# Expert slots in halves by token tile: two row halves of the array sum side by side, empty slots are not gathered

## The chip, the cores and the metric

One core of one Trainium2 chip. The metric is the device time of one execution in microseconds (us), the median over the runs of a kernel. Batch 1, 512 tokens of 1024 numbers behind 16 learned meta tokens, all in fp32.

## What is computed

One block of a hybrid encoder: input layer norm, a combined projection with two recurrent branches, output projection and layer norm, then the mixture of experts, which the change touches:

```python
scores = jax.nn.sigmoid((xt @ router_w).astype(jnp.float32))
_, idx = jax.lax.top_k(scores + router_bias, TOP_K)              # 6 of 64 experts
s_sel = jnp.take_along_axis(scores, idx, axis=-1)
wts = s_sel / jnp.sum(s_sel, axis=-1, keepdims=True) * ROUTED_SCALE
y = sum over the 6 of  wts_e * ((silu(x @ w_gate_e) * (x @ w_up_e)) @ w_down_e)  + swiglu(xt, ws_...)
h = layer_norm(DEEPNORM_ALPHA * h + y, ln2_g, ln2_b)
```

D_EXPERT is 256, so an expert has 3 MiB of weights (gate and up 1024x512, down 256x1024), and all are read. 512 x 6 = 3072 (token, expert) assignments are made.

## The kernel before

The kernel runs in four stages. The front (to some 515 us of the profile) is the projection and the two branches and isn't touched but for where small tiles lie. Routing (`out_and_route`, 515 to 609 us) makes the output projection, the norm, the shared expert (L1010, L1024) and the plan of the experts. The experts (`experts`, 609 to 1157 us) are a loop. The last norm stands at the end.

**Items and slots.** Work on experts is cut into items of 64 slots (SLOTS). An expert gets one item, and a further one for each 64 tokens beyond the first 64. Two items make a pair (PAIR): their 128 slots are the 128 partitions. Pairs run one after the other, three buffers deep (THIRDS); a pair is called p. The loop's body (`one` on each engine) is written three times and runs `n_rounds` times.

**Routing.** A token's place within its expert is a running count over all tokens (L1047 and L1048 on PE, bank PO). DVE turns places and counts into `pw`, the number of further items (L1181 to L1187), and then into tables for 112 possible items: `slot_of` (which slot a token has in an item, L1204) and `table` (three bf16 parts of the weight and two of the token number, L1211 to L1213). PE fills the time with the shared expert. The first look-up (L838) needs the table, the shared down projection (L1024) needs `shared_aT` (L1192), which stands behind the table on DVE.

**A pair in the loop.** In the order in which PE has it:
- `gate_up` (L1298): 16 matmuls of 512 columns in fp32, two items side by side, each in 64 columns of the array. Each fp32 matmul has two records in the profile (two passes), so 32.
- `turn_x` (L864): 8 transposes of the gathered rows `xg` of the next pair. ACT copies them (L872).
- `turn_a` (L1307): 2 transposes of the activations.
- `scatter` (L1322, L1323): the outputs of the pair before are added up by token. ST (128 slots x 512 tokens, ones and zeros, built by DVE at L1405) is the stationary operand: for each of 4 token tiles t and each half m of the columns, one matmul of y_hi and one of y_lo (fp32r, one pass) into one of five PSUM banks (SUM). DVE adds each of the 8 sums into `acc` (L1416) and gives the bank back (`sum_free`). The fourth sum also waits for `xgT_ready`, since its bank is one that the transposes used.
- `look_up` (L838): 4 small bf16 matmuls that find token number and weight of the slots of pair p + 3. DVE sums them up (L846 to L851, `look_free`, `idx_ready`).
- `down` (L1331): 8 fp32 matmuls of 512 columns, two items side by side in 64 columns each, 16 records.

GpSimd gathers 128 rows of 4 KiB for pair p + 3 from `h1_rows` in memory with an indirect DMA (L857). A slot without a token has token number 0 and weight 0: row 0 is fetched for it. SyncE loads the weights, six DMAs of 1 MiB for a pair (L776), each as soon as `gate_up` or `down` of the pair three before has freed its place.

After the loop a last scatter runs; ACT makes total and squares of each token tile when it is summed (L1392, L1394), DVE normalises (L1474, L1478), and SyncE stores.

## Time and profile before

| | us |
|---|---|
| median of three runs | 1182.53 |
| the three runs | 1187.83, 1182.53, 1177.49 |
| the profiled execution | 1177.19 |
| its span (first to last instruction) | 1175.4 |
| granted TensorE clock, mean | 0.994 |
| PE busy | 1128.4 (96%) |
| DVE busy | 744.1 (63%) |
| DMA read and written | 248 GB/s over the span, 420 GB/s in the loop |

A line of the profile names the line of the kernel, engine, operation and tiles, then the number of records. PE is TensorE's matmuls, PEld its weight loads. Ends of matmuls are modelled: the start of the next one tells how long one held the array. Transfers are not part of an engine's busy time. The chain of waits is the path back from the last instruction.

### The profile page before, as it was taken

What the parts mean: (1) busy time and instruction counts of PE and PEld (TensorE: products, weight loads), DVE (VectorE), ACT (ScalarE), POOL (GpSimd) and SP (SyncE); (2) the same over time, 40 slices, a digit from 0 to 9 for tenths busy, and PEclk for the clock granted to TensorE, in tenths of its full rate; (3) what the DMA queues carried; (4) which work ended last, traced back from release to release, by engine and by line L of the source; (5) the groups of instructions that cost most, each with busy time, mean ns of one, the idle gap of its engine ahead of it and who ended that gap; (6) DMA issues with size and microseconds to landing.
All of it is one profiled execution on the core that took longest, in us unless ns stands there. A gap on an engine that the chain in (4) does not pass through costs nothing.

```text
span 1175.4 us, 17834 instructions
## 1 busy us (share of the span) xinstructions
PE 1128.4 (96%) x6340; PEld 726.2 (62%) x6340; DVE 744.1 (63%) x1253; ACT 443.0 (38%) x692; POOL 204.7 (17%) x108
## 2 busy tenths in 40 slices
PE   5999999999999999999999999999999999999993
PEld 4878888888888888646544444444444454444441
DVE  8868585858586867674544555555555555555557
ACT  7656565766575657302002122211221122211224
POOL 1433242424243424100010000000000000000000
PEclk9999999999999999999999999999999999999997
DMA  6121212212121303139179999999999999999981
GB/s 235 43 107 47 102 61 86 74 74 90 57 103 44 122 26 132 47 130 400 70 314 421 419 420 422 420 421 421 421 421 421 421 421 421 422 420 421 421 352 71
DMA packets 48294, 292.08 MB, mean 248 GB/s; under 512 B 7680, under 2 KB 9088, under 8 KB 16528
## 3 DMA queue, kind: packets, MB, share of 16 engines
q1 hardware_dynamic: 43088, 272.91, 56.9%
q0 software_dynamic: 5184, 18.88, 4.0%
q8 instruction: 13, 0.21, 0.1%
q14 instruction: 9, 0.07, 0.0%
HBM read 287.57 MB, written 4.19 MB: 248 GB/s over the span
## 4 chain that ended last, share of the span: by engine, by line
PE 53%; DVE 1%; DMA 1%; ACT 1%; issue 0%; DVEq 0%; POOLq 0%
PE pair L1298 20%; PE pair L1331 11%; PE pair L1322 5%; PE pair L1323 5%; PE pair L864 3%; PE pair L1010 2%; PE pair L162 2%; PE pair L1307 1%; DMA xg<-h_rows,idx 1%; PE pair L1003 1%; DVE acc L1474 0%; ACT first L1394 0%; PE pair L997 0%; PE pair L838 0%; PE pair L1024 0%
## 5 line engine op out<-in xcount | busy, mean ns | idle before, releaser
L368 PE MATMUL pair<-hT,w_parts 128*128 128x264 f32 (+1 forms) x2112 | 376.2, 338 | 2.0 <-DVE hT L628 1.6
L368 PEld LDWEIGHTS pair<-hT,w_parts 128*128 128x128 f32 x2112 | 319.9, 188 | 47.9 <-issue 4.1
L215 POOL TENSOR_TENSOR w_parts<-w_raw,w_parts 128x1024 fp32r<-128x1024 f32 x66 | 167.2, 2535 | 307.0 <-ACT w_parts L209 295.5
L1416 DVE TENSOR_TENSOR acc<-acc,pair 128x512 f32<-128x512 f32 x280 | 170.6, 682 | 32.5 <-PE pair L1323 32.5
L1298 PE MATMUL pair<-raw,xgT 128*64 128x512 f32 x768 | 168.9, 592 | 0.0
L857 POOL DMA_INDIRECT xg<-h_rows,idx x36 | 33.9, 942 | 596.6 <-DVE idx L851 596.6
L1377 ACT ACTIVATE y_hi<-pair,w_now 128x512 fp32r<-128x512 f32 x70 | 48.1, 687 | 208.9 <-PE pair L1331 208.9
L1298 PEld LDWEIGHTS pair<-raw,xgT 128*64 128x64 f32 x768 | 55.1, 137 | 109.8 <-issue 109.8
L1408 DVE TENSOR_TENSOR act_a<-act_s,pair 128x256 f32<-128x256 f32 x35 | 14.7, 421 | 168.2 <-ACT act_s L1370 168.2
L1322 PE MATMUL pair<-y_hi,ST 128*128 128x512 f32 x280 | 112.6, 402 | 1.6 <-DVE y_lo L1429 1.6
L1323 PE MATMUL pair<-y_lo,ST 128*128 128x512 f32 x280 | 109.4, 391 | 0.0
L1370 ACT ACTIVATE act_s<-pair 128x256 f32<-128x256 f32 x35 | 13.4, 383 | 219.9 <-PE pair L1298 219.9
L1331 PE MATMUL pair<-raw,aT 128*64 128x512 f32 x384 | 87.7, 598 | 0.0
L1429 DVE SCALAR_TENSOR_TENSOR y_lo<-pair,w_now,y_hi 128x512 fp32r<-128x512 f32 x70 | 52.6, 751 | 43.0 <-ACT y_hi L1377 31.1
L1298 PE MATMUL pair<-first,xgT 128*64 128x512 f32 x352 | 77.4, 592 | 0.0
L209 ACT ACTIVATE w_parts<-w_raw 128x1024 fp32r<-128x1024 f32 x67 | 70.3, 1050 | 0.0
L1322 PEld LDWEIGHTS pair<-y_hi,ST 128*128 128x128 f32 x280 | 52.7, 188 | 12.8 <-DVE y_lo L1429 2.5
L1323 PEld LDWEIGHTS pair<-y_lo,ST 128*128 128x128 f32 x280 | 52.7, 188 | 10.1
L162 PE MATMUL pair<-w_raw,merged 128*128 128x512 f32 x128 | 55.6, 593 | 1.8 <-DVE acc L1125 1.6
L1298 PEld LDWEIGHTS pair<-first,xgT 128*64 128x64 f32 x352 | 25.3, 137 | 50.2 <-issue 50.2
L864 PEld LDWEIGHTS pair<-ident,xg 128*128 128x128 f32 x288 | 34.9, 194 | 30.4 <-issue 30.4
L695 DVE SCALAR_TENSOR_TENSOR xc<-xr,par,xc 128x528 f32<-128x528 f32 x24 | 51.8, 2157 | 0.6
(269 smaller groups left out, 1287.9 us busy)
## 6 DMA issues: line engine op xcount, KB each, us to landing
raw<-in_w_gate_up SPq DMA_DIRECT2D x96, 1024.0 KB
raw<-in_w_down SPq DMA_DIRECT2D x48, 1024.0 KB
first<-in_w_gate_up SPq DMA_DIRECT2D x44, 1024.0 KB, 25.7
w_raw<-in_w_in SPq DMA_DIRECT2D x36, 1024.0 KB, 6.7
first<-in_w_down SPq DMA_DIRECT2D x22, 1024.0 KB
xin<-in_x SPq DMA_DIRECT2D x4, 512.0 KB, 5.2
ws_gu<-in_ws_gate_up SPq DMA_DIRECT2D x1, 2048.0 KB, 7.8
h_rows<-acc SPq DMA_DIRECT2D x4, 512.0 KB, 21.1
```

Of the source, the lines that this page charges most:

```text
L162: return pe.matmul(banks[2 * (t % 2) + n][:, :], mem["merged"][:, j, t * P:(t + 1) * P], mem["w_raw"][:, j // 2, j % 2, n * 512:(n + 1) * ...
L209: act.activation(w[:, n % PARTS, 0], w_raw[:, n // 2, n % 2], ACT.Copy).then_inc(sem("w_hi_ready"), 1)
L215: pool.tensor_tensor(w[:, n % PARTS, 1], w_raw[:, n // 2, n % 2], w[:, n % PARTS, 0].bitcast(F32), ALU.subtract).then_inc(sem("w_lo_ready" ...
L368: last = pe.matmul(o, w[:, n % PARTS, pw, k * P:(k + 1) * P], hT[ph][:, k, of], start=(k == 0 and m == 0), stop=(k == KB - 1 and m == 2))
L695: ins = v.scalar_tensor_tensor(xc[:], xr[:, i:i + TA], c(C_W0 + i), xc[:], ALU.mult, ALU.add)
L864: last = pe.transpose(self.XT[k // 4][:, (k % 4) * P:(k % 4 + 1) * P], self.xg[b][:, k::KB], self.mem["ident"][:])
L1298: last = pe.matmul(GU[half[s], :], xgT[:, (KB // 2) * c + k, half[s]], w[s][:, k * 2 * F:(k + 1) * 2 * F], start=(c == 0 and k == 0), stop ...
L1322: pe.matmul(o, st, y_hi[:, m * 512:(m + 1) * 512], start=True, stop=False)
L1323: pe.matmul(o, st, y_lo[:, m * 512:(m + 1) * 512], start=False, stop=True)\
L1331: last = pe.matmul(Y[m][half[s], :], aT[:, j, half[s]], w[s][:, j * D + m * 512:j * D + (m + 1) * 512], start=(j == 0), stop=(j == 1))
L1416: v.tensor_tensor(part, part, SUM[g % len(SUM)], ALU.add).then_inc(sem("sum_free"), 1)
L1429: v.scalar_tensor_tensor(y_lo[:, cols], Y[m], w_now[:, 0:1], y_hi[:, cols].bitcast(F32), ALU.mult, ALU.subtract).then_inc(sem("y_ready"), 1)
```

## The change

**Halves.** The 64 slots of an item become a lower and an upper half of 32 (HALF). Places count up from 0 in the lower half, and from UPPER = 1024 in the upper one. A token of the first token tile (t = 0) always lies in a lower half, one of the last (t = 3) always in an upper half; tiles 1 and 2 fill what is left. The items of an expert are as many as the largest of its tokens / 64, its tokens of tile 0 / 32 and its tokens of tile 3 / 32 ask for, rounded up. `items_of` works that out on DVE, from three counts that PE makes with five more matmuls into TOT, and again for the count of items (own_tot). Possible items become 136 instead of 112.

**Order of the slots.** A pair's 128 partitions are now half by half: 32 lower slots of item 0, 32 lower of item 1, then the two upper. The transposes write their columns in an order that puts an item's 64 slots side by side again for `gate_up`, and `turn_a` turns them back. `down` therefore works on four groups of 32 columns of the array (16 matmuls, 32 records) instead of two of 64.

**Scatter.** Tile 0 needs only the partitions 0 to 63 of ST and y, tile 3 only 64 to 127. Their sums are matmuls over 64 rows each, issued in turns (SUMS: tile 0 LOW beside tile 3 HIGH, for m = 0 and m = 1). Tiles 1 and 2 stay as they were. Sums are made and reported two by two (`sum_done` += 2 behind the last of four matmuls), and the wait for `xgT_ready` is at the third sum instead of the fourth. The token tiles end in the order 0, 3, 1, 2 (TILES).

**Empty slots.** Token numbers are kept with FAR = 4096 subtracted; FAR is added at the end, so an empty slot has index 4096, and the gather, which now has a bounds check, leaves it out. GpSimd clears the three `xg` buffers once, during routing.

**Look-up.** DVE multiplies the looked-up numbers with a mask of whose slots they are and makes three operations over 128 partitions of what were four over 64. `build` is two operations of half the width.

```diff
-EXTRA = T * TOP_K // SLOTS
+HALF = SLOTS // 2
+EXTRA = 2 * P * TOP_K // HALF + (T - 2 * P) * TOP_K // SLOTS
...
     def build(self, v, b, item):
-        v.tensor_tensor(self.Sb[b][:], row.broadcast_to([P, TT, PAIR, SLOTS]),
-                        at.broadcast_to([P, TT, PAIR, SLOTS]), ALU.is_equal).then_inc(self.sem("S_built"), 1)
+        for h in range(2):
+            row = self.mem["iota"][:, h * HALF:(h + 1) * HALF].rearrange("p (t u s) -> p t u s", t=1, u=1)
+            v.tensor_tensor(self.Sb[b][:, :, h], row.broadcast_to([P, TT, PAIR, HALF]),
+                            at.broadcast_to([P, TT, PAIR, HALF]), ALU.is_equal).then_inc(self.sem("S_built"), 1)
...
-        for s in range(PAIR):
-            v.tensor_reduce(self.idx_f[b][half[s], :], GU[half[s], s * TAB + 3:s * TAB + TAB], AX, ALU.add)\
-             .then_inc(sem("idx_summed"), 1)
-        v.tensor_reduce(self.w_next[b][half[0], :], GU[half[0], 0:3], AX, ALU.add)
-        v.tensor_reduce(self.w_next[b][half[1], :], GU[half[1], TAB:TAB + 3], AX, ALU.add).then_inc(sem("look_free"), 1)
-        v.wait_ge(sem("idx_summed"), PAIR * p + PAIR)
-        v.tensor_copy(self.idx[b][:], self.idx_f[b][:]).then_inc(sem("idx_ready"), 1)
+        v.tensor_tensor(self.looked, GU[:, 0:PAIR * TAB].rearrange("p (u n) -> p u n", u=PAIR), self.of_item,
+                        ALU.mult).then_inc(sem("look_step"), 1)
+        v.wait_ge(sem("look_step"), 2 * p + 1)
+        v.tensor_reduce(self.idx_f[b], self.looked[:, :, 3:TAB], mybir.AxisListType.XY, ALU.add)\
+         .then_inc(sem("look_step"), 1)
+        v.tensor_reduce(self.w_next[b], self.looked[:, :, 0:3], mybir.AxisListType.XY, ALU.add)\
+         .then_inc(sem("look_free"), 1)
+        v.wait_ge(sem("look_step"), 2 * p + 2)
+
+        v.tensor_scalar(self.idx[b], self.idx_f[b], FAR, None, ALU.add).then_inc(sem("idx_ready"), 1)
...
         pool.indirect_dma_start(self.xg[b][:], None, self.mem["h1_rows"],
-                                bass.IndirectOffsetOnAxis(ap=self.idx[b][:, 0:1], axis=0))\
+                                bass.IndirectOffsetOnAxis(ap=self.idx[b], axis=0),
+                                bounds_check=T - 1, oob_is_err=False)\
...
+        for n, of in numbers:
+            for t in of:
+                last = pe.matmul(TOT[:, n * E:(n + 1) * E], ones[:], chosen[:, t, 0], start=(t == of[0]), stop=(t == of[-1]))
...
+        def items_of(to, n012, n3, n0):
+            st(v.tensor_tensor(to, n012, n3, ALU.add))
+            st(v.scalar_tensor_tensor(to, to, 0.5, n0, ALU.mult, ALU.max))
+            st(v.tensor_tensor(to, to, n3, ALU.max))
+            st(v.tensor_scalar(to, to, (HALF - 0.5) / 2, ROUNDER, ALU.add, ALU.add))
+            st(v.tensor_scalar(to, to, -ROUNDER, float(HALF), ALU.add, ALU.max))
...
+    LOW, HIGH = slice(0, PAIR * HALF), slice(PAIR * HALF, P)
+    SUMS = ((0, 0, LOW), (TT - 1, 0, HIGH), (0, 1, LOW), (TT - 1, 1, HIGH)) + \
+        tuple((t, m, slice(0, P)) for t in range(1, TT - 1) for m in range(2))
+    TILES = (0, TT - 1, 1, 2)
+    SHARED = 2
...
-            for g in range(ADDS):
-                t, m = g // 2, g % 2
-                o, st = SUM[g % len(SUM)], ST[b][:, t * P:(t + 1) * P]
+            for g in range(0, ADDS, 2):
+                now = SUMS[g:g + 2]
                 if g == SHARED and next_x:
                     pe.wait_ge(sem("xgT_ready"), 2 * p + 4)
-                if g >= len(SUM):
-                    pe.wait_ge(sem("sum_free"), ADDS * p + g - len(SUM) + 1)
-                pe.matmul(o, st, y_hi[:, m * 512:(m + 1) * 512], start=True, stop=False)
-                pe.matmul(o, st, y_lo[:, m * 512:(m + 1) * 512], start=False, stop=True)\
-                  .then_inc(sem("sum_done"), 1)
+                for i in range(2):
+                    if g + i >= len(SUM):
+                        pe.wait_ge(sem("sum_free"), ADDS * p + g + i - len(SUM) + 1)
+                for part in (y_hi, y_lo):
+                    for i, (t, m, of) in enumerate(now):
+                        last = pe.matmul(SUM[(g + i) % len(SUM)], ST[b][of, t * P:(t + 1) * P],
+                                         part[of, m * 512:(m + 1) * 512], start=(part is y_hi), stop=(part is y_lo))
+                last.then_inc(sem("sum_done"), 2)
...
-                    for s in both:
-                        last = pe.matmul(Y[m][half[s], :], aT[:, j, half[s]],
-                                         w[s][:, j * D + m * 512:j * D + (m + 1) * 512],
-                                         start=(j == 0), stop=(j == 1))
+                    for n in range(2 * PAIR):
+                        rows = slice(n * HALF, (n + 1) * HALF)
+                        last = pe.matmul(Y[m][rows, :], aT[:, j, rows],
+                                         w[n % PAIR][:, j * D + m * 512:j * D + (m + 1) * 512],
+                                         start=(j == 0), stop=(j == 1), tile_position=(0, n * HALF))
```

**PE, the scatter of one pair in the loop, before.** pair0 to pair3 are PSUM tiles of two banks; L1322 reads y_hi, L1323 y_lo; a REGISTER_ALU row is where a wait's number is made.

```order
L1322 MATMUL pair3<-y_hi_1969,ST0_1971 128x512
L1323 MATMUL pair3<-y_lo_1970,ST0_1971 128x512
L1322 MATMUL pair3<-y_hi_1969,ST0_1971 128x512
L1323 MATMUL pair3<-y_lo_1970,ST0_1971 128x512
L1322 MATMUL pair0<-y_hi_1969,ST0_1971 128x512
L1323 MATMUL pair0<-y_lo_1970,ST0_1971 128x512
L1319 REGISTER_ALU
L1322 MATMUL pair1<-y_hi_1969,ST0_1971 128x512
L1323 MATMUL pair1<-y_lo_1970,ST0_1971 128x512
```

**PE, the same place after.** The first two rows are the pair of sums in row halves (tile 0 beside tile 3), the last ones are whole sums of tile 1.

```order
L1404 MATMUL pair3<-y_hi_1959,ST0_1961 128x512 x2
L1404 MATMUL pair3<-y_lo_1960,ST0_1961 128x512 x2
L1398 REGISTER_ALU
L1404 MATMUL pair0<-y_hi_1959,ST0_1961 128x512
L1404 MATMUL pair1<-y_hi_1959,ST0_1961 128x512
L1404 MATMUL pair0<-y_lo_1960,ST0_1961 128x512
L1404 MATMUL pair1<-y_lo_1960,ST0_1961 128x512
L1401 REGISTER_ALU
L1404 MATMUL pair1<-y_hi_1959,ST0_1961 128x512
L1404 MATMUL pair3<-y_hi_1959,ST0_1961 128x512
L1404 MATMUL pair1<-y_lo_1960,ST0_1961 128x512
L1404 MATMUL pair3<-y_lo_1960,ST0_1961 128x512
```

The wait for the transposed x moved from behind three sums to behind two, and a sum's low part now stands behind the high part of its neighbour.

**DVE, routing, from the table's constant part to the places, before.** `pw` holds places and weights, `tot` and `need` the new counts.

```order
L1177 CAST table<-tok 128x448 x2
L1179 MEMSET base 128x112
L1181 SCALAR_TENSOR_TENSOR pw<-pair,chosen 128x4x64 [waits place_done]
L1185 COPY cnt<-pair 128x1 [waits count_done]
L1186 TENSOR_SCALAR tmp<-steps_1985,cnt 128x12 [waits route_step]
L1187 TENSOR_REDUCE cnt<-tmp 128x1 [waits route_step]
```

**DVE, the same place after.**

```order
L1229 COPY tot<-pair 128x192 [waits place_done]
L1222 TENSOR_TENSOR need<-tot 128x64 [waits route_step]
L1223 SCALAR_TENSOR_TENSOR need<-need,tot 128x64 [waits route_step]
L1224 TENSOR_TENSOR need<-need,tot 128x64 [waits route_step]
L1225 TENSOR_SCALAR need<-need 128x64 [waits route_step]
L1226 TENSOR_SCALAR need<-need 128x64 [waits route_step]
L1232 TENSOR_TENSOR need<-need,tot 128x64 [waits route_step]
L1235 TENSOR_TENSOR tie<-pair,need 128x256 [waits route_step]
L1236 TENSOR_SCALAR need<-need 128x64 [waits route_step]
L1237 TENSOR_TENSOR tie<-tie,need 128x256 [waits route_step]
L1238 TENSOR_TENSOR tie<-tie,pair 128x256 [waits route_step]
L1239 SCALAR_TENSOR_TENSOR pw<-tie,chosen 128x4x64 [waits route_step]
```

Eleven operations, each waiting for the one before it, stand where one stood; then own_tot takes seven where three stood. The four-part table behind them has 544 columns instead of 448.

## Rows read from the trace of the kernel before

**Rows 1.** The page: busy time of PE; DMA in 40 slices.

```profile
PE 1128.4 (96%) x6340; PEld 726.2 (62%) x6340; DVE 744.1 (63%) x1253; ACT 443.0 (38%) x692; POOL 204.7 (17%) x108
...
DMA  6121212212121303139179999999999999999981
```

**Rows 2.** The chain in order of time (start us, us): first, middle, last pairs.

```profile
684.20 6.87 PE pair L1298 x32
...
914.52 3.58 PE pair L1331 x16
918.10 6.87 PE pair L1298 x32
...
1136.44 6.87 PE pair L1298 x32
...
1148.44 3.61 PE pair L1331 x16
```

**Rows 3.** Waits of PE on a DMA: us in total, times, longest.

```profile
PE pair L864 <- DMA xg<-h_rows,idx: 1.2, 1, 1.2
```

**Rows 4.** Timeline of one pair (start us, us, engine, line, operation).

```profile
909.83 0.42 DVE L1408 TENSOR_TENSOR act_a<-act_s,pair 128x256 f32<-128x256 f32 x1 [4.81 <-ACT act_s L1370]
910.04 1.08 ACT L872 ACTIVATE xgT<-pair 128x512 f32<-128x512 f32 x2 [0.25 <-PE pair L864]
...
910.50 0.48 PE L1322 MATMUL pair<-y_hi,ST 128*128 128x512 f32 x1
...
910.81 0.40 PE L1323 MATMUL pair<-y_lo,ST 128*128 128x512 f32 x1
...
911.24 4.87 DVE L1416 TENSOR_TENSOR acc<-acc,pair 128x512 f32<-128x512 f32 x8 [0.93 <-PE pair L1323]
...
914.03 0.39 PE L1323 MATMUL pair<-y_lo,ST 128*128 128x512 f32 x1
914.26 0.26 PE L838 MATMUL pair<-table,Sb 128*128 x4
914.45 3.65 PE L1331 MATMUL pair<-raw,aT 128*64 128x512 f32 x16
```

**Rows 5.** Timeline of PE: matmuls over the whole array, and over row halves.

```profile
517.13 14.00 PE L162 MATMUL pair<-w_raw,merged 128*128 128x512 f32 x32 [1.61 <-DVE acc L1125]
...
478.15 1.11 PE L442 MATMUL pair<-sc,vt 64*128 64x64 f32 x16
479.19 2.00 PE L445 MATMUL pair<-q_st,S 128*128 128x64 f32 x16
```

**Rows 6.** The page: issues of the down weights.

```profile
raw<-in_w_down SPq DMA_DIRECT2D x48, 1024.0 KB
...
first<-in_w_down SPq DMA_DIRECT2D x22, 1024.0 KB
```

**Rows 7.** Windows, DMA share and GB/s last: the loop, and where the weights end.

```profile
596.00:1108.00 512.00, 510.08 (x2530) 246.32 (x2531) 276.44 (x616) 100.94 (x194) 31.86 (x34) 1.00 1.01 420
...
1140.00:1142.00 2.00, 2.00 (x12) 0.72 (x10) 0.00 (x0) 0.00 (x0) 0.00 (x0) 1.00 0.64 258
```

**Rows 8.** Timeline of routing: PE, DVE and POOL.

```profile
580.76 10.57 PE L1010 MATMUL pair<-h1T,ws_gu 128*128 128x512 f32 x24
...
567.50 0.17 DVE L1187 TENSOR_REDUCE cnt<-tmp 128x1 f32<-128x12 f32 x1
574.08 0.69 DVE L1192 TENSOR_TENSOR shared_aT<-shared_aT,pair 128x512 f32<-128x512 f32 x1 [6.42 <-PE pair L1010]
...
580.87 0.95 DVE L1204 TENSOR_SCALAR slot_of<-pair 128x448 f32<-128x448 f32 x1 [4.76 <-PE pair L1071]
...
588.98 1.15 DVE L1213 CAST table<-left 128x448 bf16<-128x448 f32 x1
591.44 0.69 DVE L1192 TENSOR_TENSOR shared_aT<-shared_aT,pair 128x512 f32<-128x512 f32 x1 [1.30 <-PE pair L1010]
...
594.86 1.11 POOL L857 DMA_INDIRECT xg<-h_rows,idx  x1 [103.95 <-DVE idx L851]
```

More of the change, by code:

```diff
@@ L939, in out_and_route @@
     gate_first = (0, 2, 1, 3)
-    R, PO, W_, SM = banks[0], banks[1], banks[6], banks[7]
+    R, PO, SM = banks[0], banks[1], banks[7]
+    spread = lambda pr: pr[:, :].rearrange("p (b c) -> p b c", b=2)[:, :, 0:2 * ITEMS].rearrange("p b (t i) -> p b t i", t=2)
+    of_tile = lambda k, t: banks[2 * k + t // 2][:, t % 2 * ITEMS:(t % 2 + 1) * ITEMS]
+    TOT = banks[1][:, TT * E:(TT + 3) * E]
+    numbers = ((0, (0, 1, 2)), (1, (TT - 1,)), (2, (0,)))
+    ROW = 2 * ITEMS
     @block.sync
@@ L1049, in _ @@
         last.then_inc(sem("place_done"), 1)
-        for t in range(TT):
-            last = pe.matmul(SM[:, 0:1], chosen[:, t].rearrange("p a e -> p (a e)"), ones[:, 0:1],
-                             start=(t == 0), stop=(t == TT - 1))
+        for n, of in numbers:
+            for t in of:
+                last = pe.matmul(SM[:, n:n + 1], chosen[:, t].rearrange("p a e -> p (a e)"), ones[:, 0:1],
+                                 start=(t == of[0]), stop=(t == of[-1]))
         last.then_inc(sem("count_done"), 1)
@@ L1055, in _ @@
         pe.wait_ge(sem("further_ready"), 1)
-        pe.matmul(SM[:, 1:2], before2[:], cnt[:, 1:2], start=True, stop=True).then_inc(sem("start_done"), 1)
+        pe.matmul(SM[:, 3:4], before2[:], cnt[:, 1:2], start=True, stop=True).then_inc(sem("start_done"), 1)
         pe.wait_ge(sem("pw_ready"), 1)
@@ L1220, in _ @@
         st(v.tensor_scalar(q2[:, 18:19], q2[:, 17:18], float(ROUNDS_MIN), None, ALU.add))
-        v.tensor_copy(mem["rounds"][:], q2[:, 18:19]).then_inc(sem("tables_read"), 1)
+        v.tensor_copy(mem["rounds"], q2[:, 18:19]).then_inc(sem("tables_read"), 1)
+        v.wait_ge(sem("pool_step"), 2 * PAIR + 1)
         for b in range(THIRDS):
-            pairs.looked_up(v, b, b)
+            pairs.looked_up(v, b, b, b == 0)
         v.wait_ge(sem("h1_stored"), 16 * TT)
@@ L1231, in _ @@
     def _(pool):
+        pool.wait_ge(sem("mix_done"), TT)
+        pool.memset(pairs.of_item, 0.0).then_inc(sem("pool_step"), 1)
+        pool.wait_ge(sem("pool_step"), 1)
+        for h in range(2):
+            for u in range(PAIR):
+                at = HALF * (PAIR * h + u)
+                pool.memset(pairs.of_item[at:at + HALF, u], 1.0).then_inc(sem("pool_step"), 1)
+        pool.wait_ge(sem("pool_step"), 2 * PAIR + 1)
+        for b in range(THIRDS):
+            pool.memset(pairs.xg[b][:], 0.0).then_inc(sem("pool_step"), 1)
+        pool.wait_ge(sem("pool_step"), 2 * PAIR + 1 + THIRDS)
         for b in range(THIRDS):
@@ L1277, in _ @@
         sp.dma_start(b2, a["norm_rows"][5:6].broadcast_to([P, D])).then_inc(sem("ln2_here"), 16)
-        for t in range(TT):
-            for part in parts(t):
-                sp.wait_ge(sem("out_ready"), t + 1 + (part.start > 0))
+        for i, t in enumerate(TILES):
+            for part in parts(i):
+                sp.wait_ge(sem("out_ready"), i + 1 + (part.start > 0))
                 sp.dma_start(out[t * P:(t + 1) * P, part], acc[:, t, part]).then_inc(sem("stored"), 16)
@@ L1462, in _ @@
         last = THIRDS * n_rounds + 2
-        for t in range(TT):
-            for m in range(2):
-                add_one(last, 2 * t + m)
-            if t == 2:
+        for g in range(ADDS):
+            add_one(last, g)
+            if g == 5:
                 mean(0)
```

152 lines of the change are left out of this document (87 added, 65 removed).

## Prediction

> **What bounds the kernel now.** I read the page first: PE is busy for 96% of the span, and the DMA line stands at 9 from the middle almost to the end [rows 1]. Two resources look full there, so the question is which one the other waits for. The list of waits of PE answers it: its only wait on a transfer is 1.2 us, once, for the first gathered rows [rows 3]. In the chain of waits the loop is PE alone, pair after pair: gate_up starts at 684.20 and, 29 pairs later, at 1136.44 [rows 2], so a pair takes 452.24 / 29 = 15.594 us. The windows show how close the second bound is: over 596 to 1108 us the DMA engines are used at 1.01 of their time with 420 GB/s [rows 7]. A pair asks for 6 MiB of weights and 0.5 MiB of gathered rows, 6.82 MB, which at 420 GB/s is 16.2 us. So the transfers fall behind by 0.6 us a pair and live on the lead of the three buffers; they end at about 1141 us, while PE begins the last down at 1148.44 [rows 2, 7]. PE sets the time, with 7 us or a little more to the other bound.
>
> How many pairs: 48 + 22 loads of down weights are 70 items [rows 6], 35 pairs, 11 rounds of three and two before.
>
> **The sum is made against the profiled execution**, 1177.2 us with a span of 1175.4. The median of the three runs is 5.3 us more; I add that at the end. A measurement of this kernel can tell about 1%, 12 us, from no change.
>
> **Part 1, scatter.** Before, from the first y_lo matmul to the last, 14 steps take 914.03 - 910.81 = 3.22 us, 0.230 each [rows 4]. That matmuls over row halves do run beside each other is in the trace: 16 records of L442 over 64 rows take 1.11 us, 16 of L445 over the whole array 2.00 [rows 5]. So tile 0 and tile 3 now take 4 steps instead of 8, and 4 x 0.230 = 0.92 us a pair is what the change seems to win. It doesn't arrive, for three reasons.
> - DVE adds the 8 sums in 4.87 us, 0.61 each (the last ends 0.07 after its step) [rows 4], and there are five banks. The third block of sums needs one bank back, the fourth block needs three. Before, the adds began at 911.24, 0.74 behind the first matmul.
> - Each change of the array's division costs. L442 has 8 steps side by side of 0.11 (L445: 2.00 less a modelled tail of 0.2, over 16), 0.9 us, but L445 starts 1.04 behind it [rows 5]: 0.14 for the change. The first matmul behind it also shows its weight load: 910.50 to 910.81 is 0.31 instead of 0.23 [rows 4]. I take 0.1 + 0.1. From turn_a into row halves and from there to whole sums are two changes more.
> - xgT_ready comes when ACT's 1.08 us from 910.04 are over, 911.12 [rows 4]. The second block now needs it; before, the fourth sum did, at about 912.
>
> Step by step, on the clock of that pair: row halves start at 910.67 instead of 910.50 (change); their y_lo at 911.00; reported at 911.40, so the adds begin at 911.43, 0.19 late. Second block 911.26 to 911.72. First bank back at 911.43 + 0.68 = 912.11, third block 912.16 to 913.18. Three banks back at 911.43 + 2 x 0.61 + 0.68 = 913.33, fourth block from 913.36, four steps and a bare load: 914.38. Before, look_up began at 914.26 [rows 4]. So +0.12 us a pair: all of the 0.92 goes into waits for DVE and changes of division.
>
> The Trainium skill speaks to the second reason. TensorEngine Tiling (Array Packing), Key Properties, says that changing the tiling mode drains the array. The trace agrees, with the 0.14 us above.
>
> **Part 2, down.** Twice the records, 32. Two groups of 64 columns run side by side: 32 records of L1298 take 6.87 us in the chain, 0.215 each, and 32 of L162 over the whole array 14.00, 0.43 each [rows 2, 5]. Four groups of 32 columns are not in the trace. Bounds: all four at once, 8 steps of 0.43, 3.44 us, as now; or still only two at once, 16 steps, 6.87 us, +3.43 a pair. Below nothing it can't go, since each group streams the same 512 columns in two passes. I take the first, since two groups show no loss at all (0.215 is half of 0.43), in rows as in columns. But down and gate_up had the same division (gate_up followed with no gap: 914.52 + 3.58 = 918.10 [rows 2]), and now there is a change: +0.14.
>
> The Trainium skill is less sure. TensorE: Matmul & The Clock Gate, Measured speedup vs the span model, gives 2.38 times for three column tiles. By that share, an estimate from that page, four give 3.2 times, down 4.3 us, and the kernel some 30 us more. The 2.0 times that two tiles show here doesn't support it; it stands inside rival B.
>
> **Part 3, the rest of a pair.** DVE: one build more, a multiply for two reductions fewer. It sits idle 4.81 us before L1408 in each pair [rows 4], which hides it. look_free gets no later than the shifted adds make it, and PE asks for it only at gate_up. GpSimd's instruction stays. Permuted transposes have as many columns. The gather: 36 gathers of 128 slots are 4608, 3072 are filled, 1536 rows of 4 KiB, 6.3 MB or 15 us of transfer at 420 GB/s, fall away. No wait of PE is on them, so that is worth nothing now: it only pushes the second bound away (6.65 MB a pair, 15.8 us).
>
> **So a pair costs 0.12 + 0.14 = 0.26 us more, x 33 pairs = 8.6 us.**
>
> **Part 4, routing.** Five matmuls for TOT and one for the counts, two records each at the 0.11 of L445, are 1.3 us of PE ahead of shared_up(1). The places take eleven dependent operations on DVE instead of one, some 3.5 us more, and the counts four more. Before, DVE was done at 567.67 and then idle for 6.42 us, until 574.08 [rows 8]: hidden. Then the table: from 580.87 to 590.13 DVE works through 448 columns, 9.3 us [rows 8]. With 544 columns and six builds for three I get 9.3 x 1.2 = 11.1, beginning 1.4 late: 593.4. PE's cover, shared_up up to 591.17 [rows 8], is over at 592.5. So DVE takes the path, and shared_aT is ready at 594.1 instead of 592.13: +2.0, carried to tables_read, to the first gather and to the first gate_up. The first gather, a third smaller, may give back a little: +1.9. The clearing of xg is hidden in GpSimd's 103.95 us without work [rows 8].
>
> **Part 5, the end.** The last scatter has the same changes: +0.2 to +0.3. The means begin behind the sixth add as before.
>
> **Sum.** 1177.2 + 8.6 + 1.9 + 0.3 = 1188.0; with the 5.3 to the median, 1193. That is 0.9% more than 1182.5. The parts that are uncertain are the changes of division: at 0.05 for all, a pair gains or loses nothing and the kernel is 2 us slower; at 0.3 each, a pair costs 0.7 us more, 25 us.
>
> **Rivals.**
> - **A, the array wins its 0.92 us (faster).** If DVE's adds and the changes didn't bind, a pair would take 15.59 - 0.92 + 0.3 = 15.0, 33 pairs 20 us less. The transfers, 15 us shorter and begun 1.9 later, then end near 1128, and the last down can't begin much before: 1148.44 - 1129 = 19 us at most. Both give 1177 - 19 + 2 = 1160, as a median 1165. For it speaks the four steps saved; against it 0.61 us an add with three banks owed. It decides only if an add took under 0.45 us. 5%.
> - **B, four groups don't run at once (slower).** Each fp32 matmul has two passes, and four groups need PE to reach past three waiting second passes. If it reaches past one only, down takes 6.87: 34 x 3.43 = 117 us, 1310. Halfway, 30 to 60 us. For it: no such row in the trace. Against: two groups have no loss. 10%.
> - **C, changes of division are hidden in the waits for banks.** Then a pair stays at 15.6, +2 to +4: median 1186. 15%.
> - **D, more items than before.** A tile over 32 tokens of one expert would add items, a round costs 3 x 15.6 = 47 us. By the reference's inputs the largest count of tile 0 is 25, of tile 3 24, and 69 items are needed either way: excluded but for an error of mine, 1%.
>
> **How the numbers follow.** The forecast (+5 to +25 us) has 69%, A 5, B 10, C 15, D 1. Its middle is at +11, just under the 12 that can be told. Same: C and half of the forecast, 0.50. Slower: the other half, B and D, 0.45. Faster: A, 0.05. The range leaves out B, D and most of A: 1180 to 1213.
>
> **What would show it.** In the profile after: a pair in the chain of 15.7 to 16.0 us, and the steps between gate_ups as above. L1404 with 16 records a pair, of which PE waits for DVE's acc (L1416's successor) before the third and fourth block. L1414 with 32 records in some 3.5 us; 6.9 would be B. A first gate_up near 610.8. Gathered bytes of 12.6 MB instead of 18.9, a DMA share still near 1 but ending 10 us or more before the last down. I would be wrong if a pair took less than 15.5 us, or if PE waited for weights.

## The result and the profile after

| | before | after |
|---|---|---|
| median (us) | 1183.82 (1177.49 to 1187.83, 6 runs) | 1193.76 (1189.02 to 1195.73, 6 runs) |
| ratio after / before | | 1.0078, 95% interval 1.0044 to 1.0111 |
| profiled execution | 1177.19 | 1193.73 |
| its span | 1175.4 | 1191.9 |

The changed kernel is 0.8% slower, and the interval leaves out "no change". The forecast was 1193 us.

The page of the kernel after: PE and two of its groups with their waits, the 40 DMA slices, the queue of the gathers, the issues of the down weights.

```profile
PE 1134.8 (95%) x6912; PEld 690.0 (58%) x6912; DVE 737.1 (62%) x1268; ACT 443.4 (37%) x692; POOL 209.8 (18%) x116
...
DMA  6121212212130303149089999999999999999921
...
q0 software_dynamic: 5184, 12.59, 2.8%
...
L1404 PE MATMUL pair<-y_hi,ST 64*128 64x512 f32 (+1 forms) x280 | 84.5, 458 | 11.4 <-DVE acc L1500 9.7
L1414 PE MATMUL pair<-raw,aT 128*32 128x512 f32 x768 | 87.4, 595 | 0.0
...
raw<-in_w_down SPq DMA_DIRECT2D x48, 1024.0 KB, 15.8
...
first<-in_w_down SPq DMA_DIRECT2D x22, 1024.0 KB, 16.2
```

Against [rows 1, 6]: the same 70 items; PE is as full as before, with 6.4 us more work and 572 records more; and a new entry, 9.7 us in which the scatter (L1404) waited for DVE's adds. The gathers move 12.59 MB. That is 18.9 MB (36 x 128 rows of 4 KiB) less a third.

The chain of waits, after, in order of time (start us, us): one pair in the middle, and the starts of gate_up from which the pair is measured.

```profile
675.19 7.02 PE pair L1376 x32
...
687.52 3.57 PE pair L1414 x32
691.09 7.02 PE pair L1376 x32
...
1152.27 7.02 PE pair L1376 x32
```

From 691.09 to 1152.27 are 29 pairs: 15.903 us each, against 15.594 [rows 2]. gate_up took 6.87 in the chain before and takes 7.02; down (32 records instead of 16) 3.58 and now 3.57.

The timeline of one pair, after (start us, us, engine, line; in brackets what ended the idle time), beside [rows 4]:

```profile
937.33 1.09 ACT L898 ACTIVATE xgT<-pair 128x512 f32<-128x512 f32 x2 [0.25 <-PE pair L885]
...
937.96 0.50 PE L1404 MATMUL pair<-y_hi,ST 64*128 64x512 f32 x2
...
938.30 0.40 PE L1404 MATMUL pair<-y_lo,ST 64*128 64x512 f32 x2
...
938.74 3.68 DVE L1500 TENSOR_TENSOR acc<-acc,pair 128x512 f32<-128x512 f32 x6 [1.14 <-PE pair L1404]
938.81 0.40 PE L1404 MATMUL pair<-y_lo,ST 64*128 64x512 f32 x2
...
939.48 0.73 PE L1404 MATMUL pair<-y_hi,ST 128*128 128x512 f32 x2 [0.27 <-DVE acc L1500]
...
940.67 0.73 PE L1404 MATMUL pair<-y_hi,ST 128*128 128x512 f32 x2
...
941.71 0.26 PE L852 MATMUL pair<-table,Sb 128*128 x4
```

The scatter starts at 937.96 and look_up at 941.71: 3.75 us, as long as before. The blocks in row halves are done early, at 939.2 (the last of them starts at 938.81 and takes 0.40). Then PE waits until DVE has given a bank back (939.48), and for the next block until three are back (940.67). What was saved stands there as idle time.

To see what a pair pays where, I took from the traces, over the 31 pairs from the fourth gate_up to the last, the mean from the first record of each group to the first of the next:

| us | turn_a to scatter | scatter | down | gate_up | pair |
|---|---|---|---|---|---|
| before | 0.193 | 3.753 | 3.484 | 6.967 | 15.594 |
| after | 0.367 | 3.750 | 3.571 | 7.019 | 15.902 |
| difference | +0.174 | -0.003 | +0.087 | +0.052 | +0.308 |

The rest of the pair (turn_x 1.01, look_up 0.187) didn't change. The experiments below are read by the same columns.

**The 16.5 us between the two profiled executions** are these (starts of the first mixing add, of the first and of the last gate_up, and the end):

| part | before | after | difference |
|---|---|---|---|
| to the first add of the output projection | 515.85 | 520.48 | +4.6 |
| routing, to the first gate_up | 93.0 | 93.9 | +1.0 |
| 34 pairs | 527.5 | 537.8 | +10.3 |
| from the last gate_up to the end | 39.1 | 39.7 | +0.6 |

The first line is not the change. Windows of the kernel after (us, PE, PEld, DVE, ACT, POOL busy, granted clock, DMA share, GB/s):

```profile
0.00:20.00 20.00, 7.71 (x39) 6.71 (x40) 16.03 (x44) 10.09 (x14) 3.59 (x6) 0.94 0.87 333
20.00:60.00 40.00, 36.59 (x220) 31.43 (x219) 32.84 (x56) 31.17 (x44) 14.96 (x7) 0.98 0.11 36
60.00:120.00 60.00, 58.16 (x397) 50.10 (x396) 42.76 (x48) 36.34 (x52) 20.80 (x9) 0.97 0.20 74
...
1171.00:1173.00 2.00, 1.72 (x5) 1.34 (x6) 2.00 (x4) 0.54 (x1) 0.00 (x0) 0.62 0.00 0
```

The granted clock was 0.94, 0.98 and 0.97 in the first 120 us; the profile of before has 1.00 in all three. The shares that are missing come to 20 x 0.06 + 40 x 0.02 + 60 x 0.03 = 3.8 us. And before_down_four (below), whose front is that of the kernel before, reaches that point at 520.3 us; the kernels with the changed front do at 516.7 (all_rows) to 524.6 (whole_first). So this point varies from execution to execution, and one pair of profiles overstates the change; the medians are 9.9 us apart.

### The profile page after: what moved, and what is told of

The parts are those of the page before. It is cut to its first block, busy times and chain, and to the rows that moved or that the text cites. A ratio compares the mean times of both kernels' runs of the same rounds, so it can differ in the third digit from the quotient of the medians.

```text
span 1191.9 us, 18995 instructions
## 1 busy us (share of the span) xinstructions
PE 1134.8 (95%) x6912; PEld 690.0 (58%) x6912; DVE 737.1 (62%) x1268; ACT 443.4 (37%) x692; POOL 209.8 (18%) x116
## 2 busy tenths in 40 slices
DMA packets 48295, 285.85 MB, mean 240 GB/s; under 512 B 9088, under 2 KB 10624, under 8 KB 16528
## 3 DMA queue, kind: packets, MB, share of 16 engines
q0 software_dynamic: 5184, 12.59, 2.8%
## 4 chain that ended last, share of the span: by engine, by line
PE 50%; DVE 4%; DMA 1%; ACT 1%; issue 0%; POOLq 0%; DVEq 0%
PE pair L1376 21%; PE pair L1414 10%; PE pair L1404 9%; PE pair L885 3%; PE pair L170 2%; DVE acc L1500 2%; PE pair L1044 1%; PE pair L1387 1%; DMA xg<-h_rows,idx 1%; PE pair L1037 1%; DVE acc L1558 0%; DVE table L1268 0%; PE pair L1031 0%; ACT first L1477 0%; PE pair L852 0%
## 5 line engine op out<-in xcount | busy, mean ns | idle before, releaser
L1460 ACT ACTIVATE y_hi<-pair,small 128x512 fp32r<-128x512 f32 x70 | 48.1, 688 | 214.8 <-PE pair L1414 214.8
L1404 PE MATMUL pair<-y_hi,ST 64*128 64x512 f32 (+1 forms) x280 | 84.5, 458 | 11.4 <-DVE acc L1500 9.7
L1414 PE MATMUL pair<-raw,aT 128*32 128x512 f32 x768 | 87.4, 595 | 0.0
L1513 DVE SCALAR_TENSOR_TENSOR y_lo<-pair,small,y_hi 128x512 fp32r<-128x512 f32 x70 | 52.6, 751 | 54.1 <-ACT y_hi L1460 54.1
L1404 PE MATMUL pair<-y_lo,ST 64*128 64x512 f32 (+1 forms) x280 | 72.4, 397 | 0.0
L1404 PEld LDWEIGHTS pair<-y_hi,ST 64*128 64x128 f32 (+1 forms) x280 | 34.3, 186 | 55.4 <-DVE acc L1500 39.7
L898 ACT ACTIVATE xgT<-pair 128x512 f32<-128x512 f32 x72 | 39.1, 595 | 28.1 <-PE pair L885 28.1
## 6 DMA issues: line engine op xcount, KB each, us to landing
raw<-in_w_down SPq DMA_DIRECT2D x48, 1024.0 KB, 15.8
first<-in_w_gate_up SPq DMA_DIRECT2D x44, 1024.0 KB, 18.9
first<-in_w_down SPq DMA_DIRECT2D x22, 1024.0 KB, 16.2
```

The lines of the kernel that those rows point to most:

```text
L1404: last = pe.matmul(SUM[(g + i) % len(SUM)], ST[b][of, t * P:(t + 1) * P], part[of, m * 512:(m + 1) * 512], start=(part is y_hi), stop=(par ...
L1414: last = pe.matmul(Y[m][rows, :], aT[:, j, rows], w[n % PAIR][:, j * D + m * 512:j * D + (m + 1) * 512], start=(j == 0), stop=(j == 1), ti ...
L1460: act.activation(y_hi[:, m * 512:(m + 1) * 512], Y[m], ACT.Copy, scale=w_now)\
L1513: v.scalar_tensor_tensor(y_lo[:, cols], Y[m], w_now, y_hi[:, cols].bitcast(F32), ALU.mult, ALU.subtract).then_inc(sem("y_ready"), 1)
```

## The experiments

My theory from the trace: +0.31 a pair is paid for changes of the array's division alone, +0.17 on the way into row halves and +0.14 at the two ends of down; the four steps that row halves save are lost again in waits for DVE. The rival: down in four groups is slower in itself, or the array's row halves never saved anything.

### down_two_groups and before_down_four: the price of down

down_two_groups is the changed kernel with down as it was (half of the slots get another item's output; the work is the same in size):

```diff
-                    for n in range(2 * PAIR):
-                        rows = slice(n * HALF, (n + 1) * HALF)
-                        last = pe.matmul(Y[m][rows, :], aT[:, j, rows], w[n % PAIR][...], tile_position=(0, n * HALF))
+                    for s in both:
+                        last = pe.matmul(Y[m][half[s], :], aT[:, j, half[s]], w[s][...])
```

> The changed kernel with down on two groups of 64 columns again (8 matmuls, 16 records a pair). The two items' outputs are mixed up in half of the slots, the work is the same in size. Theory (the change of division between down and gate_up costs, four groups of 32 stream at full rate): a pair takes 15.75 us instead of 15.905, gate_up in the chain 6.87 again instead of 7.02, and down stays at 3.5 to 3.6. Rival (something else in the loop, DVE or the gather, costs the 0.31 us a pair): the pair stays at 15.9.

before_down_four is the kernel before with down in four groups of 32 columns, two to an item:

```diff
-                    for s in both:
-                        last = pe.matmul(Y[m][half[s], :], aT[:, j, half[s]], w[s][...])
+                    for n in range(4):
+                        rows = slice(n * 32, (n + 1) * 32)
+                        last = pe.matmul(Y[m][rows, :], aT[:, j, rows], w[n // PAIR][...], tile_position=(0, n * 32))
```

> The kernel before with down alone on four groups of 32 columns. Theory: a pair takes 15.594 + 0.15 = 15.75 us, all of it at the borders of down; down itself 3.5 to 3.6 with 32 records. Rival (the order of slots or the scatter is needed for the loss): 15.6.

| us | turn_a to scatter | scatter | down | gate_up | pair | time, one run |
|---|---|---|---|---|---|---|
| down_two_groups | 0.367 | 3.750 | 3.484 | 6.968 | 15.766 | 1188.66 |
| before_down_four | 0.193 | 3.752 | 3.571 | 7.018 | 15.730 | 1186.62 |

Four groups at down cost 0.136 a pair in either kernel, and nothing else in the pair moves. The times are of one run each; the columns carry the reading. The chain of waits of down_two_groups shows both gate_up and down with their old lengths [rows 2]:

```profile
939.14 3.58 PE pair L1413 x16
942.73 6.87 PE pair L1376 x32
```

And of before_down_four:

```profile
937.57 3.57 PE pair L1332 x32
941.13 7.02 PE pair L1298 x32
```

gate_up has the same 32 records in both. It holds PE 0.15 longer in the chain where it follows four groups of 32 columns (the starts alone put 0.087 of that to down and 0.052 to gate_up; the ends of matmuls are modelled). So the price looks like one of the border, not of the sums; whole_first_32 below takes the border out and settles it.

### scatter_whole: the price of the row halves

The scatter as it was, on the new slots:

```diff
-    SUMS = ((0, 0, LOW), (TT - 1, 0, HIGH), (0, 1, LOW), (TT - 1, 1, HIGH)) + \
-        tuple((t, m, slice(0, P)) for t in range(1, TT - 1) for m in range(2))
-    TILES = (0, TT - 1, 1, 2)
-    SHARED = 2
+    SUMS = tuple((t, m, slice(0, P)) for t in range(TT) for m in range(2))
+    TILES = (0, 1, 2, 3)
+    SHARED = 3
...
```

The part left out puts back the loop over single sums, each with its own report to DVE.

> The changed kernel with the scatter of before: eight sums over all 128 rows one by one, tiles in the order 0, 1, 2, 3, the wait for the transposed x at the fourth. All else as changed. Theory (side-by-side sums win nothing, they cost 0.16 us a pair by changes of division and waits for banks): a pair takes 15.75 us, the kernel 5 us less than the changed one, 1188 or ratio 1.004 to before. Rival (row halves do win something and down loses it all): a pair gets longer, up to 15.905 + 0.9.

1187.19 us (1185.66 to 1189.98, 7 runs) against 1181.48: ratio 1.0051, interval 1.0031 to 1.0071. A pair takes 15.734, turn_a to scatter is 0.193 again, scatter 3.757, down and gate_up as after. So the row halves as built cost 0.168 a pair against whole sums: 0.174 on the way into them, and nothing won or lost inside the scatter. The rest of the loss, 34 x 0.14 + 1.0 = 5.8 us, is there without any row half: the ratio says 6.0.

### light_adds: does DVE take the win?

Adds over half of the columns. The kernel leaves out the other half of every sum, so it is a measurement and not a variant to use:

```diff
-            v.tensor_tensor(part, part, SUM[g % len(SUM)], ALU.add).then_inc(sem("sum_free"), 1)
+            v.tensor_tensor(part[:, 0:256], part[:, 0:256], SUM[g % len(SUM)][:, 0:256], ALU.add).then_inc(sem("sum_free"), 1)
```

> The changed kernel with each of DVE's adds over 256 of the 512 columns; the other half of each sum is left out. Theory (five banks and adds of 0.61 us hide the array's gain): the waits of the scatter for DVE go (9.7 us in the changed kernel), scatter shrinks to 12 steps of 0.23 and two changes of division, a pair to 15.2 to 15.3 us, the kernel by about 20 us to 1173 or so, now under the kernel before. Rival (changes of division alone eat the gain): the pair stays above 15.7. Second rival (transfers bind first): PE waits for weights, the pair stays at 15.8.

1173.48 us (1173.41 to 1174.96, 5 runs), ratio 0.9938, interval 0.9916 to 0.9959: faster than before. The timeline of one scatter:

```profile
910.41 0.50 PE L1404 MATMUL pair<-y_hi,ST 64*128 64x512 f32 x2
...
911.19 1.41 DVE L1500 TENSOR_TENSOR acc<-acc,pair 128x256 f32<-128x256 f32 x4 [1.14 <-PE pair L1404]
911.26 0.40 PE L1404 MATMUL pair<-y_lo,ST 64*128 64x512 f32 x2
...
911.66 0.73 PE L1404 MATMUL pair<-y_hi,ST 128*128 128x512 f32 x2
...
912.70 0.62 PE L1404 MATMUL pair<-y_hi,ST 128*128 128x512 f32 x2
...
913.62 0.26 PE L852 MATMUL pair<-table,Sb 128*128 x4
```

Four adds take 1.41, 0.35 each. The fourth block follows the third after 1.04 us (912.70 - 911.66) instead of 1.19, the third starts 1.25 behind the first block instead of 1.52, and scatter takes 3.206 (mean), 0.55 less. So the win of the row halves is real and DVE takes it. But it is 0.55, not 0.92: the first step in row halves, with its bare load, takes 0.34 us, and the last one before whole sums 0.40 (part of it may be the wait for the first bank, which is back at about 911.55), where a plain step takes 0.23. The pair is 15.391: 0.55 won, 0.17 + 0.14 paid, 0.04 for a wait for weights (0.8 us, once, in the 33rd of the 35 pairs). That is longer than the 15.2 to 15.3 expected; without that wait it is 15.36.

### all_rows and light_adds_all_rows: what the shorter gather is worth

Empty slots fetch the last row instead of none:

```diff
-        v.tensor_scalar(self.idx[b], self.idx_f[b], FAR, None, ALU.add).then_inc(sem("idx_ready"), 1)
+        v.tensor_scalar(self.idx[b], self.idx_f[b], FAR, T - 1.0, ALU.add, ALU.min).then_inc(sem("idx_ready"), 1)
```

> The changed kernel, but an empty slot gets row 511 (index FAR + ... cut at T - 1) instead of being left out of the gather; its weight is still 0. Theory (transfers are not what PE waits for, the gather's saving is worth nothing in the changed kernel): a pair stays at 15.90 us, the kernel within 1 us by its loop; 18.9 MB gathered instead of 12.6, the last weights land some 13 us later and still before the last down. Rival (the smaller gather helps): a pair or the last pairs get longer, PE shows waits for raw or first.

> light_adds (each add over 256 of 512 columns) with all rows gathered as in all_rows. A pair of light_adds took 15.39 us; with the whole gather a pair asks for 6.82 MB, 16.2 to 16.3 us at 418 to 420 GB/s. Before, at 15.59 us a pair, the transfers lost 0.6 us a pair (20 us) of their lead and kept 7; so the lead is some 27 us. Theory (the second bound stands close, and leaving out rows is what keeps it away): 33 pairs x 0.9 = 30 us, the lead ends in the last pairs, PE waits 3 to 6 us for weights, the kernel 3 to 6 us above light_adds (1173.5), 1177 to 1180. Rival (transfers never bind): 1173.5, no wait for weights.

| | MB gathered | pair | us | 1130 to 1140 us: DMA share, GB/s |
|---|---|---|---|---|
| all_rows | 18.88 | 15.904 | 1190.29 | 1.01, 419 |
| light_adds | 12.59 | 15.391 | 1173.48 | 0.56, 232 |
| light_adds_all_rows | 18.88 | 15.469 | 1176.72 | 1.01, 422 |

In the changed kernel a third of the gather is worth nothing: 15.904 against 15.902. With light adds, 0.08 a pair, some 3 us (one run, and on another chip than light_adds), and gate_up waits for weights. The list of waits of light_adds_all_rows (total, times, longest):

```profile
PE pair L1376 <- DMA raw<-in_w_gate_up: 2.3, 4, 1.0
...
PE pair L1376 <- DMA first<-in_w_gate_up: 0.6, 1, 0.6
```

One expectation of all_rows missed: the last weights were to land some 13 us later with all rows. Windows of the kernel after, then of all_rows:

```profile
1135.00:1140.00 5.00, 5.00 (x34) 1.51 (x28) 2.56 (x5) 1.10 (x2) 0.99 (x1) 1.00 0.56 232
1140.00:1145.00 5.00, 5.00 (x28) 2.33 (x26) 0.48 (x2) 1.32 (x3) 0.00 (x0) 1.00 0.31 123
```

```profile
1135.00:1140.00 5.00, 5.00 (x25) 1.61 (x22) 0.49 (x2) 0.05 (x1) 0.00 (x0) 1.00 1.02 419
1140.00:1145.00 5.00, 4.73 (x27) 2.99 (x28) 3.50 (x8) 1.70 (x4) 0.00 (x0) 1.00 0.75 305
```

Both end at about 1145 us, and the first gate_up of all_rows was only 3.5 us earlier (610.9 against 614.4). So the 6.3 MB that are left out end the transfers some 3 us earlier, not 13 or 15. With all rows the share drops at once at the end; with rows left out it falls slowly, from 0.97 over 1125 to 1130 us to the 0.31 above. The share is a mean over 16 DMA engines. That the left-out rows are spread unevenly over them, so that some finish long before others, would fit; no run tests it.

### whole_first: the same work in an order that doesn't owe banks

If DVE takes the win because row halves deliver sums faster than it adds them, while banks are still owed, then the row halves belong at the end of a scatter: DVE begins after one sum, has worked for 1.3 us when the short blocks come, and what it has left is done beside look_up and down. It also takes the change from turn_a into row halves out, since both are then whole.

```diff
-    SUMS = ((0, 0, LOW), (TT - 1, 0, HIGH), (0, 1, LOW), (TT - 1, 1, HIGH)) + \
-        tuple((t, m, slice(0, P)) for t in range(1, TT - 1) for m in range(2))
-    TILES = (0, TT - 1, 1, 2)
-    SHARED = 2
+    SUMS = tuple((t, m, slice(0, P)) for t in range(1, TT - 1) for m in range(2)) + \
+        ((0, 0, LOW), (TT - 1, 0, HIGH), (0, 1, LOW), (TT - 1, 1, HIGH))
+    TILES = (1, 2, 0, TT - 1)
+    SHARED = 3
...
-            for g in range(0, ADDS, 2):
-                now = SUMS[g:g + 2]
+            for g in range(ADDS):
+                if g >= 4 and g % 2:
+                    continue
...
+                now = SUMS[g:g + (2 if g >= 4 else 1)]
```

> The changed kernel with another order of sums: the four whole sums (tiles 1 and 2) first and one by one, each reported when it is done, then the two pairs of row halves (tiles 0 and 3); the wait for the transposed x is at the fourth sum again; tiles end in the order 1, 2, 0, 3. Theory (banks and late reports hide the gain; whole sums ahead keep DVE fed while the short ones come when banks are back): the adds begin 0.74 us behind the first matmul as before, no change of division ahead of the scatter (0.19 again instead of 0.37), the scatter 3.3 to 3.5 us instead of 3.75, a pair 15.35 to 15.5 us, the kernel 6 us below the one before, ratio 0.995. Rival (any change of division within the scatter costs what the steps save): 15.6 to 15.9.

1175.65 us (1173.36 to 1180.72, 7 runs) against 1180.45: ratio 0.9958, interval 0.9938 to 0.9978. Turn_a to scatter is 0.193, scatter 3.353, down 3.571, gate_up 7.088, the pair 15.400. Against the changed kernel that is 0.17 won on the way in and 0.40 in the scatter, less 0.07 of waits for weights in the last pairs. The timeline of one scatter (of whole_first_b, the same kernel):

```profile
925.83 0.48 PE L1406 MATMUL pair<-y_hi,ST 128*128 128x512 f32 x1
...
926.58 3.67 DVE L1502 TENSOR_TENSOR acc<-acc,pair 128x512 f32<-128x512 f32 x6 [0.94 <-PE pair L1406]
...
927.54 0.39 PE L1406 MATMUL pair<-y_lo,ST 128*128 128x512 f32 x1
...
927.86 0.50 PE L1406 MATMUL pair<-y_hi,ST 64*128 64x512 f32 x2
...
928.52 0.50 PE L1406 MATMUL pair<-y_hi,ST 64*128 64x512 f32 x2
...
929.18 0.26 PE L852 MATMUL pair<-table,Sb 128*128 x4
```

The adds begin 0.75 us behind the first matmul, as before the change (0.74 [rows 4]), and PE takes 1.32 us from 927.86 to 929.18 for what took 8 x 0.23 = 1.84.

### whole_first_32: the border at down taken out

Now gate_up is cut into four groups of 32 columns too (an item's two halves each get the same weights), the transposes write plainly, and down and gate_up have one division again.

```diff
-                    for s in both:
-                        last = pe.matmul(GU[half[s], :], xgT[:, (KB // 2) * c + k, half[s]], w[s][...])
+                    for n in range(2 * PAIR):
+                        rows = slice(n * HALF, (n + 1) * HALF)
+                        last = pe.matmul(GU[rows, :], xgT[:, (KB // 2) * c + k, rows], w[n % PAIR][...],
+                                         tile_position=(0, n * HALF))
...
```

> whole_first, and gate_up in four groups of 32 columns too (64 records a pair instead of 32), so that down and gate_up have one division; the transposes then need no other order of columns. Theory (the 0.14 us at the border of down and gate_up is the change of division): a pair 0.14 us shorter than whole_first, 15.2 to 15.35 us, ratio 0.991. The transfers, 15.8 us a pair with 27 us of lead, still don't bind. Rival (the loss comes with the 32-column groups themselves, or twice the records cost issue time): no shorter than whole_first, or longer.

1173.89 us (1171.78 to 1177.23, 4 runs), ratio 0.9934, interval 0.9908 to 0.9959. Down is 3.457, 0.114 less, but gate_up 7.190 with its waits for weights, and the pair 15.405 as a mean: no shorter. The expectation of 15.2 to 15.35 missed. What the mean hides is shown with the next three runs.

### whole_first_b, whole_first_all_rows, whole_first_32_b: which bound is it now?

> The same kernel as whole_first, on one chip with the two others of this call, so that they can be compared. Expected from its period of 15.40 us: 5 to 7 us under the kernel before (ratio 0.995). Theory: PE and the transfers are about level here, so the two variants beside it move the time in opposite directions only as far as the transfers let them.

> whole_first, and empty slots gather row 511 as well (18.9 MB instead of 12.6 MB). In the changed kernel that cost nothing (period 15.904 against 15.902), with light adds 0.08 us a pair. If leaving rows out is worth something as soon as the pair takes about 15.4 us: 2 to 4 us slower than whole_first_b, with waits of gate_up for weights of about 2 us a few times. If it never is, the same time within 1 us.

> whole_first with gate_up in four groups of 32 columns too. The first look won 0.114 us a pair at the border and gave it back in waits for weights. Expected: within 2 us of whole_first_b, since the transfers bind. If the border's 0.14 counted in full it would be 4 to 5 us faster.

One chip, against 20 runs of the kernel before (1180.45):

| | us | ratio, 95% interval | pair |
|---|---|---|---|
| whole_first_b | 1175.03 (9 runs) | 0.9949 (0.993 to 0.9967) | 15.400 |
| whole_first_all_rows | 1178.51 (12 runs) | 0.998 (0.9967 to 0.9992) | 15.456 |
| whole_first_32_b | 1174.35 (6 runs) | 0.9944 (0.9923 to 0.9965) | 15.424 |

The list of waits of whole_first_all_rows, then that of whole_first_32_b:

```profile
PE pair L1376 <- DMA raw<-in_w_gate_up: 2.6, 4, 0.7
...
PE pair L1376 <- DMA first<-in_w_gate_up: 1.0, 2, 0.7
```

```profile
PE pair L1377 <- DMA raw<-in_w_gate_up: 3.3, 5, 0.8
...
PE pair L1377 <- DMA first<-in_w_gate_up: 2.2, 3, 0.8
```

Starts of gate_up by the timelines: two of whole_first_b and two of whole_first_32_b, with no wait between them, then two of whole_first_32 near the end:

```profile
917.61 7.09 PE L1376 MATMUL pair<-first,xgT 128*64 128x512 f32 x32
...
932.94 7.09 PE L1376 MATMUL pair<-raw,xgT 128*64 128x512 f32 x32
```

```profile
944.00 7.05 PE L1377 MATMUL pair<-raw,xgT 128*32 128x512 f32 x64
...
959.19 7.05 PE L1377 MATMUL pair<-first,xgT 128*32 128x512 f32 x64
```

```profile
1088.74 3.62 PE L1377 MATMUL pair<-raw,xgT 128*32 128x512 f32 x32
...
1093.13 3.64 PE L1377 MATMUL pair<-raw,xgT 128*32 128x512 f32 x32 [0.77 <-DMA raw<-in_w_gate_up]
...
1104.90 3.62 PE L1377 MATMUL pair<-first,xgT 128*32 128x512 f32 x32
```

A pair without a wait takes 932.94 - 917.61 = 15.33 us with the border at down and 959.19 - 944.00 = 15.19 without it. So the border's 0.14 is real, and four groups beside each other are not slower in themselves. But only the first 26 pairs or so run like that in whole_first_32. From there on a pair takes 16.16 us (1104.90 - 1088.74), and gate_up waits in its middle for the second half of its weights (0.77 us at 1093.13): the lead of the buffers is spent. In whole_first_b the same happens from the 31st pair on. The mean of 15.42 of whole_first_32_b has 5.5 us of such waits in it, 8 of them.

Leaving out the empty rows, worth nothing in the changed kernel, is worth 3.5 us in medians once the pair is 15.4 us; that the two intervals just touch makes its size rough. It agrees with the some 3 us by which the transfers end earlier. The waits of whole_first_all_rows are shorter than the 2 us expected: six, 0.7 us at most. whole_first_b is 5.4 us faster than before, and whole_first_32_b within 0.7 us of it, as expected: PE and the transfers are now about level.

## Why the prediction was right, point by point

- **PE sets the time, the transfers don't.** Held in the changed kernel: no wait for weights; all_rows. The second bound was foreseen at 15.8 us a pair without the empty rows and 16.2 with them. The 15.8 was too low: where PE waits for weights a pair takes 16.16 (whole_first_32), with rows left out. At 15.2 us a pair the transfers fall behind by about 0.97 a pair, 25 us in 26 pairs, and that is the lead of the three buffers. The error decided nothing here, since PE never got there.
- **Part 1, scatter: +0.12 forecast.** Measured: +0.174 turn_a to scatter, -0.003 in the scatter, +0.17 in all. The mechanism was right step by step: row halves were to start 0.17 later (910.67 for 910.50), the third block 1.49 behind them, the fourth 2.69, look_up 3.71. They came at 0.174, 1.52, 2.71 and 3.75. The 0.05 that the sum lacks is in small steps, 0.03 ahead of the third block and 0.02 behind the fourth. The prediction is not at one with itself here: its list of reasons takes 0.1 for a change of division, the clock of that pair 0.17. The 0.17 went into the sum, and it is what was measured. The Trainium skill's rule (TensorEngine Tiling (Array Packing), Key Properties: a change of the tiling mode drains the array) agrees with the 0.17 here; it gives no price.
- **Part 2, down: 0.00 for four groups, +0.14 for the change.** 0.087 + 0.052 = 0.139, from two experiments 0.136. That the four groups run at once is plain in the timeline of after: the weight loads of down come four at a time, every 0.43 us (at 1164.98, 1165.41, 1165.84 in its last pair). The rival's 2.38 times for three column tiles (the Trainium skill, TensorE: Matmul & The Clock Gate, Measured speedup vs the span model) doesn't hold here: 32 records in four groups take 3.57 us with the border in it, 16 in two groups 3.48, so four groups give the whole four times, as two give the whole two (0.215 us a record for 0.43).
- **Part 3: the rest of a pair nothing, the gather nothing.** Held; turn_x and look_up moved by 0.001. But the 15 us of transfer that were to fall away were some 3 (all_rows).
- **The loop: 0.26 x 33 = 8.6.** It is 0.308 a pair and 10.3 us in 34 steps. The term mis-sized is part 1, by 0.05 a pair.
- **Part 4, routing: +1.9.** It was +1.0. PE came to the last shared products 1.49 later than before (66.40 behind the first add against 64.91 [rows 8]; forecast 1.3 to 1.4). The table I put at 11.1; from 586.99 to 597.56 it took 10.57, just as long as PE's cover beside it. The rows:

```profile
586.88 10.57 PE L1044 MATMUL pair<-h1T,ws_gu 128*128 128x512 f32 x24
586.99 1.13 DVE L1261 TENSOR_SCALAR slot_of<-pair 128x544 f32<-128x544 f32 x1 [4.83 <-PE pair L1109]
...
597.56 0.78 DVE L1249 TENSOR_TENSOR shared_aT<-shared_aT,pair 128x512 f32<-128x512 f32 x1
```

  shared_aT was thus ready 1.58 later than before, not 2.0. From there to the gather's issue it is 0.22 shorter (2.51 us against 2.73: one DVE operation less), and the first gather lands in 8.93 us instead of 9.33. Together that is +0.96, of +0.98 measured. The gather's part is of this execution: in the other profiles its first landing takes 8.6 to 9.4 us with rows left out and 9.2 to 9.6 with all.
- **Part 5, the end: +0.3, was +0.6.** 0.24 of it stands ahead of the last scatter: the last pair's own border and way into row halves. PE then stood idle for 1.59 us, waiting for y_lo, as before, and over 1171 to 1173 us the granted clock was 0.62 (windows above): it fell from the higher of its two levels, 2.4 GHz, to the lower, 1.2. The last whole sums took 0.43 us a step instead of 0.23. The same place before had 1.00. In down_two_groups, with the same scatter and a clock of 1.00 there, the stretch from the last scatter to the end takes 21.77 us as before (21.76); after it takes 22.09. So 0.33 is the clock, and the row halves cost nothing there.
- **Rival A (faster by row halves).** It was right that the length of an add decides: with 0.35 us the kernel is 0.6% faster than before. No run tests its limit of 0.45 us. Its price was too high: the array wins 0.55 of the 0.92, so 1173 and not 1165.
- **Rival B (four groups not at once), C (changes hidden), D (more items)** are out: down 3.57; both changes show in full; 70 items.

The sum was right partly by luck: loop and end were 2.0 us too low, routing 0.9 too high, and the 5.3 us to the median stood on three runs. The sum of the three parts measured is 11.9, the medians say 9.9. And the profiled execution after came out at 1193.7 only because its front was 4.6 us late, a term that the sum doesn't have.

What stays open is why the way into row halves costs 0.17 from turn_a, but 0.09 behind a whole sum (927.54 to 927.86 is 0.32, a plain step 0.23), with DVE's bank named as the releaser. By DVE's adds (from 926.58, 0.61 each) the one bank that is needed was back at about 927.3, before the last whole sum's y_lo began, which speaks for the change and against the wait; no run tells them apart.

## What to carry to other kernels

Packing two short sums side by side shortens only the producer; if the consumer frees the banks at its own pace, nothing comes out but the price of the changes of division. Put the packed, fast part last in its group, behind work that lets the consumer start early: here that order, which also took the costly border away from the front of the scatter, turned 0.8% slower into 0.4 to 0.5% faster. And count the borders: here a crossing between two divisions of the array cost 0.05 to 0.17 us, so a packing should be shared by the instructions that stand next to each other. A saving in transfers that is worth nothing at first can be worth something once PE is faster. And look at the periods one by one: a bound that stands behind a lead doesn't show in the first pairs, and a mean over all of them hides it.

## What the runs showed of the hardware that I had not expected

- Four groups of 32 columns in fp32 with 512 columns each run fully beside each other: by the timelines 64 records of gate_up take 7.05 us in whole_first_32_b, and 32 records over two groups of 64 take 7.09 in whole_first_b.
- A border between groups of 32 and groups of 64 columns costs 0.14 us for the way in and out together, though both only divide columns.
- An indirect gather that leaves out rows keeps its number of packets (5184) and moves a third fewer bytes. The pages of after and of all_rows show what becomes of them: 9088 packets under 512 B against 7552, 1536 more, as many as there are empty slots (4608 - 3072).
- Those 6.3 MB less made the transfers end some 3 us earlier, where 420 GB/s would give 15 us (after against all_rows).
